# Gate and up projections: three of eight row pairs by seven block products instead of two, with the partial banks added on GpSimd

## What is computed

```python
D_FF = -(-(8 * D_MODEL) // (3 * 256)) * 256          # 5632; D_MODEL = 2048, 256 tokens
h2 = _rms_norm(x, norm2_g[l])
x = x + (jax.nn.silu(h2 @ w_gate[l]) * (h2 @ w_up[l])) @ w_down[l]
```

## Time and profile before

| quantity | value |
|---|---|
| median of 3 runs | 1955.91 us (1955.36 to 1956.25) |
| the profiled execution: its time, its span | 1956.17 us, 1954.4 us |
| PE busy, share of the span | 1940.2 us, 99% |
| DVE busy | 1365.1 us, 70% |
| ACT busy | 1000.4 us, 51% |
| POOL busy | 78.4 us, 4% |

### The profile page before, as it was taken

One profiled execution on the slowest core, in us unless ns is written; L12 is line 12 of the kernel. 1 busy time (PEld: TensorE's weight loads), 2 busy tenths in 40 slices (PEclk: granted clock), 3 DMA queues, 4 the chain that ended last, 5 costly groups with the idle time before them and its releaser, 6 DMA issues.

```text
span 1954.4 us, 26367 instructions
## 1 busy us (share of the span) xinstructions
PE 1940.2 (99%) x9560; PEld 1621.4 (83%) x9560; DVE 1365.1 (70%) x1617; ACT 1000.4 (51%) x1327; POOL 78.4 (4%) x123
## 2 busy tenths in 40 slices
PE   9999999999999999999999999999999999999999
PEld 7888888887888888888787778888888888888887
DVE  6595655556667664655657986778888888678777
ACT  6365444444555453444555555645555555445453
POOL 3000000001200000000300100000000000000000
PEclk9999999999999999999999999999999999999999
DMA  8674555665765445666465545656665666655654
GB/s 289 198 228 130 155 170 167 185 202 162 257 182 188 147 133 175 183 197 191 143 195 159 154 140 168 187 180 197 199 193 188 193 192 194 205 182 194 224 199 159
DMA packets 204474, 360.75 MB, mean 185 GB/s; under 512 B 13169, under 2 KB 53088, under 8 KB 204112
## 3 DMA queue, kind: packets, MB, share of 16 engines
q1 hardware_dynamic: 199792, 346.15, 55.8%
q0 software_dynamic: 4576, 13.20, 2.4%
HBM read 357.20 MB, written 2.10 MB: 184 GB/s over the span
## 4 chain that ended last, share of the span: by engine, by line
PE 97%; ACT 1%; DVE 1%; DMA 0%; issue 0%; DVEq 0%; ACTq 0%
PE psum L755 23%; PE psum L757 23%; PE psum L756 23%; PE psum L762 6%; PE psum L764 3%; PE psum L1302 2%; PE psum L1304 2%; PE psum L1303 2%; PE psum L1543 1%; PE psum L871 1%; PE psum L1236 1%; PE psum L885 1%; PE psum L860 1%; PE psum L1017 1%; PE psum L1793 0%; PE psum L779 0%
## 5 line engine op out<-in xcount | busy, mean ns | idle before, releaser
L720 DVE TENSOR_TENSOR wl<-raw,wh 128x1024 fp32r<-128x1024 f32 (+2 forms) x595 | 694.7, 1191 | 341.9 <-ACT wh L712 328.7
L712 ACT ACTIVATE wh<-raw 128x1024 fp32r<-128x1024 f32 (+2 forms) x595 | 603.2, 1032 | 536.3 <-PE psum L757 388.6
L755 PE MATMUL psum<-wh,xs 128*128 128x512 f32 (+2 forms) x1440 | 559.5, 389 | 4.0 <-DVE xs L1055 3.8
L757 PE MATMUL psum<-wh,xs 128*128 128x512 f32 (+2 forms) x1440 | 552.9, 384 | 0.0
L756 PE MATMUL psum<-wl,xs 128*128 128x512 f32 (+2 forms) x1440 | 552.6, 384 | 0.0
L755 PEld LDWEIGHTS psum<-wh,xs 128*128 128x128 f32 x1440 | 270.6, 188 | 60.6 <-DVE xs L1055 6.4
L757 PEld LDWEIGHTS psum<-wh,xs 128*128 128x128 f32 x1440 | 270.5, 188 | 53.2
L756 PEld LDWEIGHTS psum<-wl,xs 128*128 128x128 f32 x1440 | 270.7, 188 | 50.9
L762 PE MATMUL psum<-xs,wh 128*128 128x512 f32 x512 | 181.6, 399 | 0.0
L764 PE MATMUL psum<-xs,wl 128*128 128x256 f32 x512 | 143.4, 280 | 0.0
L755 PE MATMUL psum<-wh,mh 128*128 128x512 f32 x360 | 141.6, 393 | 0.0
(11 more groups left out here) (478 smaller groups left out, 2232.1 us busy)
## 6 DMA issues: line engine op xcount, KB each, us to landing
raw<-in_w_in_dram SPq DMA_DIRECT2D x263, 512.0 KB, 4.5
raw<-in_w_out_dram SPq DMA_DIRECT2D x96, 512.0 KB, 3.8
raw<-in_w_gate_dram SPq DMA_DIRECT2D x88, 512.0 KB, 4.1
raw<-in_w_up_dram SPq DMA_DIRECT2D x88, 512.0 KB, 4.3
raw<-in_w_down_dram SPq DMA_DIRECT2D x80, 512.0 KB, 4.6
cmp_raw<-in_cmp_w_dram SPq DMA_DIRECT2D x16, 512.0 KB, 4.5
raw<-in_w_small_dram SPq DMA_DIRECT2D x16, 336.0 KB, 3.1
bias<-in_b_in_dram POOLq DMA_DIRECT2D x18, 256.0 KB, 4.1
```

The lines of the kernel that those rows point to most:

```text
L712: act.activation(shaped(wh[:, n % SPLIT_SLOTS], unit)[:, 0:k, 0:unit.n], shaped(buffer, unit)[:, 0:k, 0:unit.n], ACT.Copy).then_inc(hi_don ...
L720: dve.tensor_tensor(out=shaped(wl[:, n % SPLIT_SLOTS], unit)[:, 0:k, 0:unit.n], in0=shaped(buffer, unit)[:, 0:k, 0:unit.n], in1=shaped(wh[ ...
L755: pe.matmul(o, ah_[:, kt, tok], hi_w, start=first, stop=False)
L757: ins = pe.matmul(o, al_[:, kt, tok], hi_w, start=False, stop=last)
```

## The change

Three pairs (1, 3 and 5) of eight are done by seven products in steps 1 to 9, instead of two (3 and 6). The order of the units in a step is new (`g` and `u` plain units of gate and up, `S` a seven, `G4` and `U4` plain units that are split and multiplied as two halves of one block each). Raw slots are assigned by a list of their own, so that a seven always has slots 0 and 1, and loads are requested in `LOAD_ORDER`. The transposes stand after the second unit of a step instead of the fourth, and into PSUM banks 6 and 7 instead of 4 and 5. DVE makes the weight sums of the step's first seven at the step's start, ahead of its third unit. The four extra banks are copied to SBUF by ACT in two instructions, and combined there by POOL in four adds; DVE adds the accumulators; ACT applies the row factor in two further passes; POOL multiplies gate by up into `act_a`.

```diff
-GATE_UP_SEVENS = (3, 6)
-GATE_UP_ORDER = ("g0", "g1", "u0", "u1", "g2", "u2", "S0", "g3", "u3", "S1", "g4", "g5", "u4", "u5")
+GATE_UP_SEVENS = (1, 3, 5)
+GATE_UP_ORDER = ("g0", "u0", "g1", "S0", "u1", "g2", "S1", "u2", "g3", "S2", "u3", "G4", "U4")
+GATE_UP_RAWS = ("S0", "g0", "u0", "S1", "g1", "u1", "S2", "g2", "u2", "G4", "U4", "g3", "u3")
+LOAD_ORDER = (2, 3, 0, 1, 6, 7, 10, 4, 5, 11, 14, 8, 9, 15, 12, 13)
...
-FIRST_SEVEN, SEVENS_END, GATE_END = 6, 16, 18
+GATE_UP.released[0] = GATE_UP.released[1] = 4
+FIRST_SEVEN, SEVENS_END, GATE_END, TURN_UNITS = 3, 19, 22, 2
...
+            def pool_mix(i):
+
+                def add(out_, a, b):
+                    return pool.tensor_tensor(out=x_mixes[:, out_, :], in0=x_mixes[:, a, :], in1=x_mixes[:, b, :],
+                                              op=ALU.add)
+                pool.wait_ge(s("act_mixes"), 3 * (i - FIRST_SEVEN_STEP) + 1)
+                stand_alone(pool, "pool")
+                add(1, 0, 1)
+                pool.drain()
+                pool.wait_ge(s("act_mixes"), 3 * (i - FIRST_SEVEN_STEP) + 2)
+                stand_alone(pool, "pool")
+                add(2, 2, 1)
+                pool.drain().then_inc(s("pool_mixes"), 1)
+                add(1, 3, 1)
+                add(3, 3, 2)
+                pool.drain().then_inc(s("pool_mixes"), 1)
+                pool.wait_ge(s("act_mixes"), 3 * (i - FIRST_SEVEN_STEP) + 3)
+                pool.wait_ge(dve_mid_done, ffn_place(i + 1).slots + 1)
+                stand_alone(pool, "pool")
+                pool.tensor_tensor(out=act_a[:, :, :], in0=x_mixes[:, 1:4:2, :], in1=silu[:, :, :], op=ALU.mult)
+                pool.drain().then_inc(s("pool_mixes"), 1)
...
-                    if n == 2:
+                    if n == 1:
                         pe.wait_ge(dve_mid_done, pl.slots + 1)
...
-                    if n == SLOT_UNITS - 1:
+                    if n == TURN_UNITS - 1:
+                        if not isinstance(i, int):
+                            pe.wait_ge(s("pool_mixes"), 3 * (i - FIRST_SEVEN_STEP))
                         pe_stage(pl, 0, turn_act)
...
-            def first_mix(pl):
+            def copy_mixes(pl):
 
                 act.wait_ge(unit_used, SPLIT_SLOTS + pl.units + SEVENS_END)
-                act.activation(x_mixes[:, 0, :], psum[:, 4, :], ACT.Copy).then_inc(s("first_mix"), 1)
+                act.activation(x_mixes[:, 0:2, :], psum[:, 4:6, :], ACT.Copy).then_inc(s("act_mixes"), 1)
+                act.activation(x_mixes[:, 2:4, :], psum[:, 6:8, :], ACT.Copy).then_inc(s("act_mixes"), 1)
...
-                    ins = act.activation(silu[:, tb, :], x_mixes[:, 2 * tb, :], ACT.Silu, scale=x_rstd[:, tb:tb + 1])
-                ins.then_inc(s("gate_ready"), 1)
+                    ins = act.activation(silu[:, tb, :], silu[:, tb, :], ACT.Silu, scale=x_rstd[:, tb:tb + 1])
+                act.drain()
+                for tb in range(TB):
+                    ins = act.activation(silu[:, tb, :], silu[:, tb, :], ACT.Copy, scale=x_rstd[:, tb:tb + 1])
+                ins.then_inc(s("act_mixes"), 1)
...
-            def gate_sum():
-                dve.drain()
-                tt(x_mixes[:, 0:3:2, :], acc[0], x_mixes[:, 0:3:2, :], ALU.add)
+            def gate_sum(i):
+                dve.wait_ge(s("pool_mixes"), 3 * (i - FIRST_SEVEN_STEP) + 1)
+                tt(silu[:, :, :], acc[0], x_mixes[:, 0:3:2, :], ALU.add)
 
             def up_of_mixes(i):
-                tt(x_mixes[:, 3:5, :], acc[1], x_mixes[:, 3:5, :], ALU.add)
-                dve.wait_ge(s("second3_rstd"), TB)
-                dve.wait_ge(s("gate_ready"), i)
-                dve.drain()
-                for tb in range(TB):
-                    dve.scalar_tensor_tensor(out=act_a[:, tb, :], in0=x_mixes[:, 3 + tb, :], scalar=x_rstd[:, tb:tb + 1],
-                                             in1=silu[:, tb, :], op0=ALU.mult, op1=ALU.mult)
+                dve.wait_ge(s("pool_mixes"), 3 * (i - FIRST_SEVEN_STEP) + 2)
+                tt(x_mixes[:, 1:4:2, :], acc[1], x_mixes[:, 1:4:2, :], ALU.add)
...
                 pl = ffn_place(i)
+                dve_mid(pl, -1, 0, up_part if isinstance(i, int) else lambda: up_of_mixes(i - 1))
+                for part in range(2):
+                    _, loaded, count = raw_buffer(pl, FIRST_SEVEN + part, GATE_UP.units[FIRST_SEVEN + part])
+                    dve.wait_ge(loaded, count)
+                    stand_alone(dve, "dve")
+                sum_weights(GATE_UP.units[FIRST_SEVEN + 1])
```

More of the change, by code:

```diff
@@ L115, in __init__ @@
         self.by_rows = False
-        self.raw = self.part = None
+        self.raw = self.part = self.half = None
 def slots_of(units):
@@ L235, in load, with raw_of, eight_in_halves @@
         return len(self.raws) - 1
+    def raw_of(self, g, kts):
+        return self.raws.index((g, kts)) if (g, kts) in self.raws else self.load(g, kts, None)
     def eight(self, g, kts, first, last):
         unit = Unit(self.weights[g], ((0, GN),), kts, "t", g, self.operand, self.ktiles, first, last)
-        unit.raw = self.load(g, kts, len(self.units))
+        unit.raw = self.raw_of(g, kts)
+        self.released[unit.raw] = len(self.units)
         self.units.append(unit)
+    def eight_in_halves(self, g, kts, last):
+        raw = self.raw_of(g, kts)
+        self.released[raw] = len(self.units) + 1
+        for half, kt in enumerate(kts):
+            unit = Unit(self.weights[g], ((0, GN),), (kt,), "t", g, self.operand, self.ktiles, False, last and half == 1)
+            unit.raw, unit.half = raw, half
+            self.units.append(unit)
     def seven(self, j):
         kts = (2 * self.pairs[j], 2 * self.pairs[j] + 1)
-        raws = [self.load(g, kts, None) for g in range(2)]
+        raws = [self.raw_of(g, kts) for g in range(2)]
         assert raws[0] % 2 == 0
@@ L284, in __init__ @@
         eights = [pair for pair in range(KT // 2) if pair not in GATE_UP_SEVENS]
+        for kind in GATE_UP_RAWS:
+            pair = (GATE_UP_SEVENS if kind[0] == "S" else eights)[int(kind[1])]
+            for g in range(2) if kind[0] == "S" else ("gu".index(kind[0].lower()),):
+                self.load(g, (2 * pair, 2 * pair + 1), None)
         for kind in GATE_UP_ORDER:
@@ L710, in split_high @@
             act.wait_ge(unit_used, place.units + n + 1)
[L711 removed]
+            k, k0 = len(unit.kts), unit.half or 0
             act.activation(shaped(wh[:, n % SPLIT_SLOTS], unit)[:, 0:k, 0:unit.n],
[L713 removed]
+                           shaped(buffer, unit)[:, k0:k0 + k, 0:unit.n], ACT.Copy).then_inc(hi_done, 1)
         def split_low(place, n, unit):
@@ L1273, in gate_up_units, with last_step_units @@
                     for i, w in enumerate(("w_gate_2", "w_up_2")) for j in range(KT // 2)]
+        def last_step_units():
+            units = gate_up_units()
+            for n, unit in enumerate(units):
+                unit.raw = n ^ 2
+            return units
         def summed_before(i, unit):
@@ L1289, in of_sum @@
             def of_sum(which):
+                if unit.operand == "x" and unit.pair == 2:
+                    return x_sum_high_2[:, which, :], x_sum_low_2[:, which, :]
                 return sum_h[:, unit.pair, which, :], sum_l[:, unit.pair, which, :]
@@ L1330, in seven_low @@
                               in1=wh[:, n % SPLIT_SLOTS, 0:k, :].bitcast(F32), op=ALU.subtract).then_inc(lo_done, 1)
-            if unit.part == 1:
+            if unit.part == 1 and not (unit.operand == "x" and unit.pair == 0):
                 sum_weights(unit)
@@ L1929, in ffn_step @@
                         h = FFN_SLOT_ENDS.index(n + 1)
+                        if h == 0 and not first:
+                            pe.wait_ge(s("pool_mixes"), 3 * N_SEVEN_STEPS)
                         pe_stage(pl, h, turn_act if h == 0 and not first else nothing)
@@ L3006, in ffn_step @@
                 pl = ffn_place(i)
-                for n, unit in enumerate(units):
+                for n, unit in enumerate(units if first else last_step_units()):
                     if n >= (SLOT_UNITS if first else AHEAD):
```

89 lines of the change are left out of this document (51 added, 38 removed).

## The result

The changed kernel takes 1997.21 us (median of 4 runs, 1996.29 to 1998.14), the kernel before on the same chip 1956.08 us (1955.36 to 1956.29). The ratio is 1.0211, with a 95% interval of 1.0199 to 1.0224: 2.1% slower, 41 us. The forecast was slower, 1973 us; the size is outside its range.

The account below looks back on a forecast made before the run. PE's list of matmuls was taken to bound the kernel. Against 0.68 us saved per step, delays of 0.4 + 1.1 + 1.4 = 2.9 us made eight loop steps 2.2 us longer: 1973 us from 1956.2, range 1951 to 1991.

Parts of the forecast that it names:

- the sum: Delays per loop step with POOL and DVE both waiting, less PE's saving: 2.2 us longer in eight steps, 1973 us.
- the adds' delay: Turn of a step: POOL's last two adds take turns with DVE's low splits, so unit 24's split begins 1.1 us later.
- the product's: Turn of a step: DVE's second weight sum waits for POOL's gate-by-up product, 1.5 us less 0.1 us of gap.
- step 1: First step with sevens, outside the eight loop steps counted as longer: saves 0.7 us.
- What bounds before, and what PE saves: PE, busy 99%, sets the time; 3 matmuls fewer in steps 1 to 9 save 0.68 us each, 6.1 us in all.
- DVE's own chain at the turn: DVE's splits, adds and weight sums, POOL costing nothing: third unit's split 0.4 us late, taken as 0 to 0.4.
- B: Moment when PE is done with the first half of G4, unit 20; times at the turn count from it.
- My first rival: No contention that matters between POOL and DVE: 2.9 to 6.1 us saved, 1950 to 1953 us; chance 0.30.
- Contention on both sides: POOL's SBUF reads and DVE's two-SBUF-input instructions make each other wait: slower, 1965 to 1991 us; chance 0.50.
- POOL's prices: POOL's adds of 512 columns and product of 1024: 0.8 and 1.5 us taken, upper end 1.4 and 2.5.
- unit 24's split: DVE's low split for the next step's first unit: ends at B + 2.53 without POOL, begins 1.1 us later with it.
- The forecast's own check: Weight sums and low splits beside POOL recorded far longer than 1.23 and 0.69 us, or starting late; otherwise prediction wrong.

Follow-up runs that it names:

- run 9: Changed kernel with POOL's four adds whole and its product cut to one column, the rest of the product left out: 1985.29 us.
- run 1: Changed kernel with POOL's four adds and product cut to one column each, the rest left out, all waits kept: 1957.06 us.
- Run 2: Changed kernel with POOL doing the same amount of reading at the same times on other data, its results needed by nobody: 1995.99 us.
- runs 6 and 7: Kernel before with POOL work added per seven step: two 1024-column products in 6, 1969.13 us; four writes of zeros, reading nothing, in 7, 1955.45 us.
- run 10: Changed kernel with POOL's product whole and its four adds cut to one column each, the rest of the adds left out: 1974.36 us.
- run 12: Changed kernel with the first seven's weight sums back behind its part 1 split, plus ten filler matmuls ending each seven step: 1996.52 us.

## Why the prediction was wrong in size

The mechanism, DVE held by POOL as well as POOL by DVE, was right. What failed is the size of three terms of the sum: the adds' delay (1.1 us forecast, 2.4 measured), the product's (1.4 against 2.0), both mostly from POOL prices of 0.8 and 1.5 us where 1.3 and 2.4 were measured, and step 1, where POOL's pause of 6.47 us was in no term.

**What bounds before, and what PE saves**: right. PE loses 27 matmuls, three in each of nine steps. With the clock kept, the 24 matmuls ahead of the transposes take 5.6 us in run 9, against 5.44 at the pitch of before.

**DVE's own chain at the turn**: half right. I had the third unit's split 0.4 us late; in run 1 it is on the edge. But I looked only at PE's wait at the third unit. PE also waits at the step's first matmul, through `pe_stage` and `dve_mid`, for the gate add. I had that add end at B + 3.85 and PE's step end at B + 4.08, and took it as met. From the add's end to the matmul it takes 0.82 us (run 1), so PE starts 0.4 us late, and 0.5 with the slower pitch behind it, even with POOL's work gone. POOL's pause takes another 2.3 us in step 1 of that run. My first rival, 2.9 to 6.1 us saved, was therefore not to be had with this order: its 0.30 should have stood with no change.

**Contention on both sides**: right. Run 2 excludes latency as the cause in the loop steps, runs 6 and 7 show it on the kernel before, for reads and not for writes. The Trainium skill, page "SBUF — State Buffer", section "Who interferes with whom", says this of both directions, and the trace agrees: 0.69 us becomes 2.69 on DVE, and a one-column POOL operation 0.19 becomes 1.24 (run 1).

**POOL's prices**: too small. I took 0.8 and 1.5 us. The rows free of DVE have 1.26 to 1.29 us for 512 columns and 2.41 for 1024, near the upper bounds I had set (1.4 and 2.5). The Trainium skill, page "GPSIMD Engine Reference", section "Performance versus the Vector engine", led to an estimate of 1.15 and 2.3 us and 1986 us; the trace agrees with these prices within 0.15 us, and the sentence that I set beside the sum was nearer than the sum.

**The delays**: the adds hold unit 24's split by 2.4 us, not 1.1 (its end is at 1520.05, where B is 1515.12 and I had B + 2.53). I had POOL's first two adds beside an idle DVE, until B - 1; the second ends at 1515.57, B + 0.45, so three adds and not two lie among the splits. The product holds the second weight sum by 2.0 us, not 1.4 (2.69 against 0.69; run 10: 17.3 us in all). With the own chain of 0.4, and 0.2 us in seams, the step is 5.0 - 0.68 = 4.3 us longer, not 2.2: 47.55 us against 45.4 forecast. In eight steps that is 17 us of the 24 us missed.

**Step 1**: I had 0.7 us saved; it is 5.4 us longer, 6.1 us more than forecast. POOL's pause of 6.47 us was in no term. By itself it accounts for 2.3 us of them (run 1, with one column per operation: 44.68 us instead of 42.37); the rest needs the full adds behind it (run 9: 48.43 us). About 1 us is left that I assign to nothing.

The forecast's own check, that weight sums and splits beside POOL would be recorded far longer, came in. Of the wait forecast at the third unit, about 3 us, 1.5 came in where the clock was kept and 0.3 to 0.5 where it fell; most of PE's waiting was at the step's first matmul.

## What to carry to other kernels

An idle engine that reads the memory that a busy one reads isn't free: price its operations by their full length on the busy engine's list, above all where that list sets when PE goes on. When work moves, list every semaphore that the waiting engine passes, not only the one you expect to be late, and take the distance from the releasing instruction's end to the first dependent start from a row. Where a saving is 0.3% and the chain around it meets within tenths, free help is needed and not only idle help.

## What the runs showed of the hardware

- A held instruction ended only after the other engine's operation had: a 0.69 us sum took 2.69 us beside a 2.4 us product, and three splits of 3.48 us took 5.69 beside the second of two products in run 6, 2.2 us more. POOL writing 1024 columns in 0.96 us held nothing, and DVE's adds with a PSUM input kept their length beside POOL's reads (2.77 us for three, run 6).
- POOL stood for 6.47 us between the first and second operation of its first pass through the steps' loop, and 6.47 again in runs 1, 9 and 10, even with one column per operation. In runs 6 and 7, on the kernel before, it stood for 6.29 and 6.27 us at the same place of its loop, for products and for writes, where it cost nothing. So it is neither the operation nor its data. The profile puts it down to "issue"; what it is was not tried.
- After equal waits of 2.45 us the granted clock was kept in some steps and fell in others (run 9, and the changed kernel), and it fell in two steps of run 10 behind a wait of 1.54 us. In run 9 each fall cost 1.6 to 1.9 us, in run 10 1.6; in the changed kernel, where DVE set the step, it cost nothing, and in run 12 keeping it gained nothing. Why it fell in one step and not in the other stays open.
